# A hybrid conv and linear-attention layer with a ConvFFN: the next tile's scores ahead of this tile's mean of squares on TensorE, and loads and low parts in another order

## The chip, the cores and the metric

One Trainium2 chip, one of its cores. The metric is the device time of one execution in microseconds. The kernel is one program with an instruction list for each engine: TensorE (PE in the profile, PEld its weight loads), VectorE (DVE), ScalarE (ACT), GpSimd (POOL) and SyncE (SP, which issues the DMAs). The engines run side by side and meet only at semaphores; each takes its own list strictly in order.

## The reference, cut to what matters

2048 prompt rows and 64 sample rows of width 1024 go through one layer. All is float32.

```python
def mixer(xn, conv_prev, gla_prev, ...):
    bg, cg, h, q, k, v, gr, r = split(xn @ w_in)
    cv, conv_new = causal_dwconv(cg * h, conv_prev, conv_w)
    y_conv = rmsnorm(bg * cv, g_conv)
    logg = log_sigmoid(gr @ w_alpha + b_alpha) / 16
    o, gla_new = gla(q / 8, k, v, logg, gla_prev)     # 4 heads
    y_gla = rmsnorm(o, g_gla) * silu(r)
    return concat([y_conv, y_gla]) @ w_out, conv_new, gla_new

def gla(q, k, v, logg, s0):                            # chunks of 64 rows
    b = cumsum(logg)                                   # inside a chunk
    qt, kt, kd = q * exp(b), k * exp(-b), k * exp(b_last - b)
    att = where(mask, qt @ kt.T, 0)                    # the scores
    s_next = exp(b_last) * s + kd.T @ v
    o = att @ v + qt @ s                               # s: the state before the chunk

x = x + mixer(rmsnorm(x, norm1))
u = rmsnorm(x, norm2) @ w_up                           # 1024 x 5632
a, g = split(causal_dwconv(u, prev, ffn_conv_w))
x = x + (silu(g) * a) @ w_down                         # 2816 x 1024
y = rmsnorm(x, final_norm)
```

## The kernel before, in words

**Split products.** A float32 operand is written as a high part (rounded to the type that TensorE takes fast) and a low part (the rest). A product is three matmuls, high by high, low by high, high by low (L1617 to L1619). For a weight ScalarE makes the high part and GpSimd the low part; a part can't be used before both are there. `wq` holds such pairs for the large products, `w_hi` and `w_lo` those for v and for the output projection.

**Seven products for eight.** The projections of the mixer and w_up are computed with seven block products (numbered 0 to 6) over sums and differences of weight quarters; VectorE makes the four weight sums of a step in `sum_up` (tile `wu_sum`, L2080 to L2086) from `wu_raw`, and adds the products in PSUM together (`r_1` by ScalarE; `r_2` at L2538 and `r_3` at L2556 by VectorE). Product 5 of a step waits for `r_3`.

**Stages.** Rows come in three blocks of 768, 768 and 580 columns. For every block: the first norm and the turning of its tiles of 128 rows (x_n to xt_hi and xt_lo), the v product ("values"), 10 pairs of projections, of which gla runs beside, then the output projection, then the second norm. After the three blocks' mixers the ConvFFN runs for all three blocks in turn, 22 steps of 128 hidden rows each, 7 products a step, with the down products between them.

**gla beside the pairs.** `mix_events` places steps X, Y and Z of a tile t between pair products. On TensorE, X is `outputs_1(t)` (L1774 to L1781) and the gate product of t+1; Y is `outputs_2(t)` (L1788) and the cumulative sums of t+1 (L1744); Z is `mean_squares(t)` (L1796, one product of a ones matrix with `o_sq`) and `scores(t+1)` (L1752, and two transposes of k_end, L1757). For Z, ScalarE squares the output of t (`o_sq`, L1317), and VectorE's `decays(t+1)` makes q_exp, k_exp (L2185) and k_end. After `mean_squares`, ScalarE takes the root (`o_rs`, L1323 and L1326), and VectorE scales the tile (`gla_out`) behind `masked_scores(t+1)` (L2193). This happens 14 times with a next tile: 5, 5 and 4 in the three blocks.

**Output projection.** It is computed in two passes p of four weight units (slots) each. A pass starts with slot 0 for four row groups, slot 1 for the same four, and so on. The low parts of its rows come per head, for the two halves of a block's columns (`low_part`, L580). In pass 0 VectorE makes heads 0 and 1 (`y_lo_first`), GpSimd heads 2 and 3 between its low parts of the weight units (L554).

**Start and change of stages.** SP's list of loads sets what lands first; the rings take what SP issues in order. At the end of the last block's mixer the first FFN step is prepared: its products are split (L1110, L997), three split operands are stored for later blocks (`w_ops`), the weights of step 1 are loaded, then w_down's, and four x_ops tiles are stored, on which ScalarE's high part of w_down (`wd_hi`, L1192) waits, since it lies on the same memory.

Of the kernel before, what the change touches and what calls it, by code (L numbers as in the profile page):

```python
# [17 lines left out]
CJ = D_CONV // P  # L18
HEADS = 4
# [192 lines left out]
def build(nc, x_prompt, x_sample, state_conv, state_gla, state_ffn, w_in, w_alpha, b_alpha, conv_w,  # L212
          g_conv, g_gla, w_out, norm1, norm2, w_up, ffn_conv_w, w_down, final_norm,
          y_prompt, y_sample, conv_prompt, gla_prompt, ffn_prompt, conv_sample, gla_sample, ffn_sample):
    with ExitStack() as ctx:
# [182 lines left out]
        def mix_counts(b):  # L398
# [11 lines left out]
                "gla_y": nt, "y_hi": nch * HEADS + CJ, "y_lo": nch * (HEADS - 2) + CJ, "y_lo_first": 2 * nch,  # L410
# [226 lines left out]
        def _(sp):  # L637
# [92 lines left out]
            for b in range(NB):  # L730
# [12 lines left out]
                for t in range(0 if b else nt):  # L743
                    n1.wait(sp, "scaled", t - NX + 1)
                    load_x(t, b)
                    if t == 0:
                        load_gain(norm1[0])
                    if t < 2:
                        for slot in (2 * t, 2 * t + 1):
                            load_unit(sp, v_unit(b, slot))  # L750
                    if t == 2:
                        with nc.allow_non_contiguous_dma(reason="small parameters"):
                            sp.dma_start(raw_gr[:, :, :], w_in_v[:, :, C_GR:C_R]).then_inc(gr_loaded, 16)
                    if t == nt - 2:
                        load_parameters()
# [73 lines left out]
                if b == NB - 1:  # L829
# [3 lines left out]

                    for i in (1, 3, 4):
                        store_op(0, i)
                    sp.wait_ge(wu_lo, splits(0, 0, 5))
                    load_up(0, 1)
# [86 lines left out]
        def _(pool):  # L924
# [16 lines left out]
            for b in range(NB):  # L941
# [25 lines left out]
                def low_heads(chunk):  # L967
                    for n in range(2, HEADS):
                        mix.wait(pool, "y_hi", HEADS * chunk + n + 1)
                        mix.inc(low_part(pool, n, *CHUNKS[b][chunk]), "y_lo")  # L970

                low_unit(pool, out_unit(b, 0))
                low_unit(pool, out_unit(b, 1))
                low_heads(0)
                low_unit(pool, out_unit(b, 2))
                low_unit(pool, out_unit(b, 3))
                low_heads(1)
# [6 lines left out]
                if b == NB - 1:  # L984
                    mix.wait(pool, "y_lo", nch * (HEADS - 2) + CJ)
# [79 lines left out]
        def _(act):  # L1065
# [136 lines left out]
            act.wait_ge(consts_ready, 9)  # L1202
            for b in range(NB):
# [33 lines left out]
                if b == 0:  # L1237
                    for t in range(nt):
                        first_rstd(b, t)
                        if t >= 1:  # L1240
                            first_high(b, t - 1)
                        for slot in ((0, 1), (2, 3), ())[min(t, 2)]:
                            high_unit(act, v_unit(b, slot))
# [367 lines left out]
        def _(pe):  # L1611
# [29 lines left out]
            for b in range(NB):  # L1641
# [157 lines left out]
                for ev in mix_events(b):  # L1799
# [24 lines left out]
                    if ev[0] == "Z":  # L1824
                        mean_squares(t)
                        if more:
                            scores(t + 1)

                def out_group(p, n, slots):
# [9 lines left out]
                    for slot in slots:  # L1839
                        pe.wait_ge(lo_ready[slot], unit_index(b, "out", slot, p) + 1)  # L1840
                        if p:
                            mix.wait(pe, "y_lo", nch * (HEADS - 2) + slot + 1)
                        else:
                            mix.wait(pe, "y_lo_first" if slot < 2 else "y_lo", 2 * chunk_of_end(b, t) + slot % 2 + 1)
# [175 lines left out]
        def _(dve):  # L2020
# [67 lines left out]
            for b in range(NB):  # L2088
# [126 lines left out]
                def first_lows(c):  # L2215

                    for n in range(2):
                        mix.wait(dve, "y_hi", HEADS * c + n + 1)
                        mix.inc(low_part(dve, n, *CHUNKS[b][c]), "y_lo_first")
# [36 lines left out]
                def pair_event(p, i):  # L2256
# [51 lines left out]
                    if (p, i) == (NPAIR - 1, 4):  # L2308
                        first_lows(0)
# [39 lines left out]
                first_lows(nch - 1)  # L2349
# [7 lines left out]
                def add_out(p, j):  # L2357
# [4 lines left out]
                    if (p, t) == (0, max(TILES) // 2):  # L2362

                        mix.wait(dve, "y_lo", nch * (HEADS - 2))
# [151 lines left out]
            def ffn_step(b, f, par, more=True):  # L2516
# [22 lines left out]
                if edge == 0 and b == 0:  # L2539
                    sum_up(g + 1, 0)  # L2540
                    sum_up(g + 1, 1)
                    low_x(b, 5)
# [15 lines left out]
                if edge == 0 and b:  # L2558
# [7 lines left out]
                if edge == 0:  # L2566
                    low_x(b, 6)
                if at_last and b + 1 == NB - 1:
# [70 lines left out]
```

## Time and profile before

| | |
|---|---|
| median of 3 runs | 2353.17 us (2353.15 to 2356.1) |
| the profiled execution | 2356.82 us, its span 2355.1 us |
| TensorE matmuls | 2262.9 us busy, 96% |
| VectorE, ScalarE, GpSimd | 1700.4, 1002.6, 1209.8 us busy |
| granted TensorE clock, mean | 0.99 |
| DMA | 412.73 MB, mean 175 GB/s |

TensorE is busy in nearly the whole span, so the time is its work plus its idle stretches. Those lie in the first 20 us, in the mixer of each block, where the FFN starts (900 to 940 us), at the two changes of blocks in the FFN (about 1400 to 1470 and 1900 to 1980 us), and in the last 20 us.

### The profile page before, as it was taken

The page shows a single profiled execution, that of the slowest core. Times are in us where ns is not written, and L with a number is a line of the kernel's source. Part 1 is how long each engine was busy: PE and PEld are TensorE (multiplying, and loading weights), DVE is VectorE, ACT ScalarE, POOL GpSimd, SP SyncE. Part 2 cuts the span into 40 slices and gives each one's busy share as a digit, 9 for nine tenths or more (in the row PEclk, how much of TensorE's full clock was granted, in tenths as well). Part 3 has the DMA queues.
Part 4 walks back from the last instruction along what each step waited for, and adds up shares of the span by engine and source line. Part 5 has one row for each costly group of instructions (what it writes and reads, how often), then busy time and mean ns, then how long its engine had stood idle before and what let it go on. Part 6 is the DMA issues. An engine that isn't in the chain of part 4 may idle for free. (4 is left out here: it accounts for less than half of the span.)

```text
span 2355.1 us, 39571 instructions
## 1 busy us (share of the span) xinstructions
PE 2262.9 (96%) x12602; PEld 2072.1 (88%) x12602; DVE 1700.4 (72%) x2516; ACT 1002.6 (43%) x1957; POOL 1209.8 (51%) x1251
## 2 busy tenths in 40 slices
PE   7999999999999997999999998999999988999997
PEld 6998888988889976999999987999999977999996
DVE  6477775377554656989898887667676687788786
ACT  4544463343634454344444445333333335444343
POOL 2654732214532357787787865444444454555552
PEclk9999999999999998999999999999999999999999
DMA  3543446535366557544445476444444457555552
GB/s 124 192 166 133 162 159 226 170 117 183 130 232 206 175 211 268 179 151 160 163 157 177 152 259 224 148 158 149 151 147 142 151 171 251 196 187 196 194 188 102
DMA packets 264595, 412.73 MB, mean 175 GB/s; under 512 B 14108, under 2 KB 186993, under 8 KB 264497
## 3 DMA queue, kind: packets, MB, share of 16 engines
q1 hardware_dynamic: 264497, 411.45, 51.5%
q8 instruction: 58, 0.95, 0.2%
q14 instruction: 40, 0.33, 0.0%
HBM read 313.24 MB, written 98.16 MB: 175 GB/s over the span
## 5 line engine op out<-in xcount | busy, mean ns | idle before, releaser
L1617 PE MATMUL ps<-xo,wq 128*128 128x384 f32 (+1 forms) x1848 | 598.6, 324 | 24.8 <-POOL wq L997 10.6
L1618 PE MATMUL ps<-xo,wq 128*128 128x384 f32 (+1 forms) x1848 | 598.1, 324 | 0.0
L1619 PE MATMUL ps<-xo,wq 128*128 128x384 f32 (+1 forms) x1848 | 597.6, 323 | 0.0
L2471 DVE TENSOR_TENSOR resid<-resid,ps 128x512 f32<-128x512 f32 (+1 forms) x728 | 477.5, 681 | 73.8 <-PE ps L1619 45.2
L997 POOL TENSOR_TENSOR wq<-wu_raw,wq 128x256 fp32r<-128x256 f32 x396 | 384.4, 994 | 103.9 <-ACT wq L1110 103.8
L1617 PEld LDWEIGHTS ps<-xo,wq 128*128 128x128 f32 x1848 | 350.2, 189 | 46.6 <-issue 14.7
L1618 PEld LDWEIGHTS ps<-xo,wq 128*128 128x128 f32 x1848 | 350.6, 190 | 20.3
L1619 PEld LDWEIGHTS ps<-xo,wq 128*128 128x128 f32 x1848 | 351.0, 190 | 0.0
L2488 DVE SCALAR_TENSOR_TENSOR up_y<-up_u,params,up_y 128x768 f32<-128x768 f32 (+1 forms) x264 | 288.0, 1091 | 48.5 <-ACT up_y L1154 29.3
L519 POOL TENSOR_TENSOR wq<-wu_raw,wq 128x256 fp32r<-128x256 f32 x174 | 146.0, 861 | 300.9 <-ACT wq L1234 300.9
L1617 PE MATMUL ps<-wd_hi,hid_hi 128*128 128x512 f32 x704 | 277.0, 393 | 11.2 <-DVE resid L2471 11.2
L1619 PE MATMUL ps<-wd_lo,hid_hi 128*128 128x512 f32 x704 | 278.1, 395 | 0.0
L1618 PE MATMUL ps<-wd_hi,hid_lo 128*128 128x512 f32 x704 | 275.2, 391 | 0.0
L1027 POOL TENSOR_TENSOR wd_lo<-wd_raw,wd_hi 128x512 fp32r<-128x512 f32 x132 | 173.4, 1335 | 159.7 <-ACT wd_hi L1192 159.7
L1021 POOL TENSOR_TENSOR hid_lo<-up_y,hid_hi 128x384 fp32r<-128x384 f32 (+1 forms) x132 | 120.2, 932 | 167.5 <-ACT hid_hi L1182 167.5
L997 POOL TENSOR_TENSOR wq<-wu_sum,wq 128x256 fp32r<-128x256 f32 x176 | 159.1, 932 | 62.2 <-ACT wq L1110 62.2
L1617 PE MATMUL ps<-w_hi,xt_hi 128*128 128x512 f32 (+1 forms) x408 | 164.9, 404 | 6.4 <-POOL w_lo L554 3.1
L1154 ACT ACTIVATE up_y<-up_u,params 128x768 f32<-128x768 f32 (+1 forms) x132 | 116.9, 886 | 127.3 <-DVE up_u L2578 89.2
L1617 PE MATMUL ps<-xt_hi,wq 128*128 128x384 f32 (+1 forms) x480 | 158.8, 331 | 4.3 <-issue 2.9
L1618 PE MATMUL ps<-w_hi,xt_lo 128*128 128x512 f32 (+1 forms) x408 | 160.4, 393 | 0.0
L1619 PE MATMUL ps<-w_lo,xt_hi 128*128 128x512 f32 (+1 forms) x408 | 160.3, 393 | 0.0
L1619 PEld LDWEIGHTS ps<-wd_lo,hid_hi 128*128 128x128 f32 x704 | 132.9, 189 | 28.5
(246 smaller groups left out, 4232.0 us busy)
## 6 DMA issues: line engine op xcount, KB each, us to landing
wq<-w_ops SPq DMA_DIRECT2D x176, 512.0 KB, 4.5
wu_raw<-in_w_up_dram SPq DMA_DIRECT2D x89, 512.0 KB, 4.0
w_ops<-wq SPq DMA_DIRECT2D x88, 512.0 KB, 2.6
wq<-m_ops SPq DMA_DIRECT2D x80, 512.0 KB, 3.9
wd_raw<-in_w_down_dram SPq DMA_DIRECT2D x66, 512.0 KB, 5.3
wu_raw<-in_w_in_dram SPq DMA_DIRECT2D x40, 512.0 KB, 4.9
m_ops<-wq SPq DMA_DIRECT2D x40, 512.0 KB, 3.1
x_in<-in_x_prompt_dram SPq DMA_DIRECT2D x32, 512.0 KB, 5.6
```

What stands on the lines that cost most here:

```text
L519: last = eng.tensor_tensor(wq[:, at, 1, r], w[:, r], wq[:, at, 0, r].bitcast(F32), ALU.subtract)
L997: last = pool.tensor_tensor(wq[:, WQ_AT[i], 1, r], src[:, r], wq[:, WQ_AT[i], 0, r].bitcast(F32), ALU.subtract)
L1021: last = pool.tensor_tensor(hid_lo[:, par, r], up_y[:, 0, r], hid_hi[:, par, r].bitcast(F32), ALU.subtract)
L1027: last = pool.tensor_tensor(wd_lo[:, par, r], wd_raw[:, r], wd_hi[:, par, r].bitcast(F32), ALU.subtract)
L1154: return act.activation(up_y[:, m, 0:w], up_u[:, m, 2:2 + w], ACT.Copy, scale=params[:, FFN_TAP + 2, bass.ds(m * NF + f, 1)])
L1617: pe.matmul(out, lh, rh, start=(first and n == 0), stop=False, skip_group_check=skip)
L1618: pe.matmul(out, ll, rh, start=False, stop=False, skip_group_check=skip)
L1619: last = pe.matmul(out, lh, rl, start=False, stop=end, skip_group_check=skip)
L2471: last = dve.tensor_tensor(resid[0:m, t, s], resid[0:m, t, s], ps[0:m, bank, :], ALU.add)
L2488: dve.scalar_tensor_tensor(y, up_u[:, m, tap:tap + w], params[:, FFN_TAP + tap, bass.ds(m * NF + f, 1)], y, ALU.mult, ALU.add).then_inc(su ...
```

## The change

Five edits.

1. `scores(t+1)` stands before `mean_squares(t)` in step Z on TensorE.
2. The first loads: x tile 1 stands before the first v unit, and x tile 2 before the other three; ScalarE's high parts of the v units are spread behind the norm steps, and its wait for the constants stands behind the first table load.
3. Output projection: VectorE makes all four heads of the first half of the columns, GpSimd all four of the second half, behind the low parts of units 0 to 3.
4. End of the last mixer, on SP: the load of w_up for step 1 stands before the stores of the split operands.
5. First FFN step, on VectorE: the weight sums of step 1 stand behind r_3, the low parts of x operands 5 and 6 and the sum of the last quarter.

```diff
@@ SP, first loads
-                    if t < 2:
-                        for slot in (2 * t, 2 * t + 1):
-                            load_unit(sp, v_unit(b, slot))
+                    for slot in {1: (0,), 2: (1, 2, 3)}.get(t, ()):
+                        load_unit(sp, v_unit(b, slot))
@@ SP, end of the last mixer
+                    sp.wait_ge(wu_lo, splits(0, 0, 5))
+                    load_up(0, 1)
                     for i in (1, 3, 4):
                         store_op(0, i)
-                    sp.wait_ge(wu_lo, splits(0, 0, 5))
-                    load_up(0, 1)
                     second[b].wait(sp, "squared", nt)
                     load_down(0)
@@ GpSimd, low parts of the output projection
-                def low_heads(chunk):
-                    for n in range(2, HEADS):
-                        mix.wait(pool, "y_hi", HEADS * chunk + n + 1)
-                        mix.inc(low_part(pool, n, *CHUNKS[b][chunk]), "y_lo")
-                low_unit(pool, out_unit(b, 0))
-                low_unit(pool, out_unit(b, 1))
-                low_heads(0)
-                low_unit(pool, out_unit(b, 2))
-                low_unit(pool, out_unit(b, 3))
-                low_heads(1)
+                for n in range(4):
+                    low_unit(pool, out_unit(b, n))
+                for n in range(HEADS):
+                    mix.wait(pool, "y_hi", HEADS + n + 1)
+                    mix.inc(low_part(pool, n, *CHUNKS[b][1]), "y_lo")
@@ ScalarE, start
-            act.wait_ge(consts_ready, 9)
...
                 if b == 0:
+                    act.wait_ge(consts_ready, 9)
                     for t in range(nt):
                         first_rstd(b, t)
-                        if t >= 1:
+                        if t == 1:
+                            high_unit(act, v_unit(b, 0))
+                        if t >= 1 and t != 3:
                             first_high(b, t - 1)
-                        for slot in ((0, 1), (2, 3), ())[min(t, 2)]:
-                            high_unit(act, v_unit(b, slot))
+                        if t == 2:
+                            high_unit(act, v_unit(b, 1))
+                            first_high(b, 2)
+                            high_unit(act, v_unit(b, 2))
+                            high_unit(act, v_unit(b, 3))
@@ TensorE, step Z
                     if ev[0] == "Z":
-                        mean_squares(t)
                         if more:
                             scores(t + 1)
+                        mean_squares(t)
@@ VectorE, low parts
-                def first_lows(c):
-                    for n in range(2):
-                        mix.wait(dve, "y_hi", HEADS * c + n + 1)
-                        mix.inc(low_part(dve, n, *CHUNKS[b][c]), "y_lo_first")
+                def first_lows(heads):
+                    for n in heads:
+                        mix.wait(dve, "y_hi", n + 1)
+                        mix.inc(low_part(dve, n, *CHUNKS[b][0]), "y_lo_first")
...
-                first_lows(nch - 1)
+                first_lows((2, 3))
@@ VectorE, FFN step
                 dve.tensor_tensor(r_2[:, 0:h], ps[:, 1, 0:h], r_1[:, 0:h], ALU.add).then_inc(r2_read, 1)
-                if edge == 0 and b == 0:
-                    sum_up(g + 1, 0)
-                    sum_up(g + 1, 1)
-                    low_x(b, 5)
...
                 adds(3)
-                if edge == 0 and b:
+                if edge == 0:
                     low_x(b, 5)
...
                 if edge == 0:
                     low_x(b, 6)
+                if first_of_all:
+                    sum_up(g + 1, 0)
+                    sum_up(g + 1, 1)
```

TensorE's list at the first step Z of block 0 (o_sq is the squared output of this tile, q_exp, k_exp and k_end are of the next), with its - and +:

```order
-L1796 MATMUL ps<-o_sq,ones 128x512 [waits mix_o_squared]
 L1752 MATMUL ps<-q_exp,k_exp 128x128 [waits mix_att_read,mix_qk_exp]
 L1752 MATMUL ps<-q_exp,k_exp 128x128 x3
 L1757 MATMUL ps<-ident,k_end 128x128 [waits mix_qk_exp]
 L1757 MATMUL ps<-ident,k_end 128x128
+L1796 MATMUL ps<-o_sq,ones 128x512 [waits mix_o_squared]
```

The mean of squares moved behind the four score products and the two transposes.

VectorE's list in the first FFN step, before (r_66 is r_2, r_79 is r_3, wu_sum the weight sums of step 1, xo the low parts of x operands 5 and 6):

```order
L2538 TENSOR_TENSOR r_66<-ps,r_65 128x384 [waits r1_read,mix_p_done]
L2080 TENSOR_TENSOR wu_sum<-wu_raw 128x512 [waits wu_lo,mix_w_loaded1,mix_w_loaded0]
L2082 TENSOR_TENSOR wu_sum<-wu_sum,wu_raw 128x512 [waits mix_w_summed]
L2084 TENSOR_TENSOR wu_sum<-wu_raw 128x512
L2086 TENSOR_TENSOR wu_sum<-wu_raw,wu_sum 128x512 [waits mix_w_summed]
L2070 TENSOR_TENSOR xo<-xo_raw,xo 128x1536 [waits xo_high]
L2556 TENSOR_TENSOR r_79<-ps,r_65 128x384 [waits later_scaled,mix_p_done]
L2508 TENSOR_TENSOR up_u<-ps,r_79 128x384 [waits r3_read,mix_p_done]
L2070 TENSOR_TENSOR xo<-xo_raw,xo 128x1536 [waits xo_high]
L2578 TENSOR_TENSOR up_u<-ps,r_65 128x384 [waits mix_p_done]
```

and now:

```order
L2538 TENSOR_TENSOR r_66<-ps,r_65 128x384 [waits r1_read,mix_p_done]
L2552 TENSOR_TENSOR r_79<-ps,r_65 128x384 [waits later_scaled,mix_p_done]
L2070 TENSOR_TENSOR xo<-xo_raw,xo 128x1536 [waits xo_high]
L2508 TENSOR_TENSOR up_u<-ps,r_79 128x384 [waits r3_read,mix_p_done]
L2070 TENSOR_TENSOR xo<-xo_raw,xo 128x1536 [waits xo_high]
L2080 TENSOR_TENSOR wu_sum<-wu_raw 128x512 [waits wu_lo,mix_w_loaded1,mix_w_loaded0]
L2082 TENSOR_TENSOR wu_sum<-wu_sum,wu_raw 128x512 [waits mix_w_summed]
L2084 TENSOR_TENSOR wu_sum<-wu_raw 128x512
L2086 TENSOR_TENSOR wu_sum<-wu_raw,wu_sum 128x512 [waits mix_w_summed]
L2577 TENSOR_TENSOR up_u<-ps,r_65 128x384 [waits mix_p_done]
```

The four sums moved from before r_79 to behind the second low part; r_79 is now next after r_66.

SP's list at the same place, with its - and + (the stores w_ops are of step 0's operands, the loads wu_raw of step 1's weights):

```order
 L708 DMA xo_raw<-x_ops 128x1536 [waits mix_out_done]
 L708 DMA xo_raw<-x_ops 128x1536
+L656 DMA wu_raw<-in_w_up_dram 128x8x128 [waits wu_lo]
+L656 DMA wu_raw<-in_w_up_dram 128x8x128
 L695 DMA w_ops<-wq 128x1024 [waits wu_lo] x3
-L656 DMA wu_raw<-in_w_up_dram 128x8x128 [waits wu_lo]
-L656 DMA wu_raw<-in_w_up_dram 128x8x128
 L712 DMA wd_raw<-in_w_down_dram 128x1024 [waits later_squared]
```

The two loads stand before the three stores.

## Rows read from the trace of the kernel before

**Rows 1.** Who TensorE waited for, whole run: total us, times, longest.
```profile
PE ps L1617 <- POOL wq L997: 10.6, 1, 10.6
PE ps L1796 <- ACT o_sq L1317: 4.4, 4, 1.7
```

**Rows 2.** Timeline of the start: start us, us, engine, line, tiles [idle before].
```profile
10.66 1.06 ACT L1069 ACTIVATE squares<-x_in 128x1024 f32<-128x1024 f32 x1 [0.22 <-DMA x_in<-in_x_prompt_dram]
...
15.13 1.05 ACT L1069 ACTIVATE squares<-x_in 128x1024 f32<-128x1024 f32 x1
...
20.39 0.78 PE L1617 MATMUL ps<-w_hi,xt_hi 128*128 128x512 f32 x1
...
22.03 1.28 DVE L2038 TENSOR_TENSOR xt_lo<-ps,xt_hi 128x512 fp32r<-128x512 f32 x2
...
24.67 0.40 PE L1617 MATMUL ps<-w_hi,xt_hi 128*128 128x512 f32 x1
```

**Rows 3.** Timeline where output projections of block 0 and block 2 begin.
```profile
269.00 0.50 PE L1617 MATMUL ps<-w_hi,xt_hi 128*128 128x512 f32 x1 [0.53 <-POOL w_lo L554]
...
829.53 2.02 POOL L580 TENSOR_TENSOR xt_lo<-gla_y,xt_hi 128x290 fp32r<-128x290 f32 x2
831.52 5.94 POOL L554 TENSOR_TENSOR w_lo<-raw,w_hi 128x512 fp32r<-128x512 f32 x4
834.81 0.50 PE L1617 MATMUL ps<-w_hi,xt_hi 128*128 128x512 f32 x1 [2.08 <-POOL w_lo L554]
```

**Rows 4.** Stretches: from:to us, length, PE busy, PEclk, DMA share, GB/s.
```profile
835.86:839.27 3.41, 3.41 (x10) 0.50 1.01 410
907.60:921.20 13.60, 5.68 (x18) 0.50 1.06 369
918.00:934.00 16.00, 13.61 (x64) 0.82 1.05 381
```

**Rows 5.** Timeline of three of the 14 steps Z, all engines.
```profile
182.93 0.60 ACT L1317 ACTIVATE o_sq<-ps 128x512 f32<-128x512 f32 x1
183.58 1.12 PE L1796 MATMUL ps<-o_sq,ones 128*128 128x512 f32 x2 [1.73 <-ACT o_sq L1317]
184.05 0.43 DVE L2185 TENSOR_TENSOR k_exp<-k_exp,qk 128x256 f32<-128x256 f32 x1
184.54 1.15 PE L1752 MATMUL ps<-q_exp,k_exp 128*128 128x128 f32 x8
...
204.30 2.02 PE L1752 MATMUL ps<-q_exp,k_exp 128*128 128x128 f32 x8 [1.65 <-DVE k_exp L2185]
...
783.07 0.43 DVE L2185 TENSOR_TENSOR k_exp<-k_exp,qk 128x256 f32<-128x256 f32 x1
```

**Rows 6.** Timeline of the first two FFN steps, VectorE, TensorE and ScalarE.
```profile
909.87 0.90 DVE L2080 TENSOR_TENSOR wu_sum<-wu_raw 128x512 f32<-128x512 f32 x1 [10.90 <-DMA wu_raw<-in_w_up_dram]
...
914.83 0.54 DVE L2556 TENSOR_TENSOR r<-ps,r 128x384 f32<-128x384 f32 x1
...
915.52 0.66 PE L1617 MATMUL ps<-xo,wq 128*128 128x384 f32 x1 [10.62 <-POOL wq L997]
...
921.69 1.05 ACT L1192 ACTIVATE wd_hi<-wd_raw 128x1024 fp32r<-128x1024 f32 x1
...
931.15 0.41 PE L1617 MATMUL ps<-xo,wq 128*128 128x384 f32 x1 [2.39 <-DVE r L2538]
...
934.49 1.00 DVE L2080 TENSOR_TENSOR wu_sum<-wu_raw 128x512 f32<-128x512 f32 x1 [3.48 <-issue]
...
938.03 0.41 PE L1617 MATMUL ps<-xo,wq 128*128 128x384 f32 x1 [0.23 <-DVE r L2556]
```

**Rows 7.** SP's issues: the w_up loads of step 1, the last x_ops store (with us to landing).
```profile
899.12 2.69 SPq L656 DMA_DIRECT2D wu_raw<-in_w_up_dram  x2
...
910.18 1.39 SPq L845 DMA_DIRECT2D x_ops<-xl_a  x1
...
x_ops<-xl_a SPq DMA_DIRECT2D x1, 580.0 KB, 9.3
```

More of the change, by code:

```diff
@@ L409, in mix_counts @@
                 "state0": nt, "state1": full, "o_squared": nt, "o_mean": nt, "o_rs": 2 * nt, "gla_step": nt,
-                "gla_y": nt, "y_hi": nch * HEADS + CJ, "y_lo": nch * (HEADS - 2) + CJ, "y_lo_first": 2 * nch,
+                "gla_y": nt, "y_hi": nch * HEADS + CJ, "y_lo": HEADS + CJ, "y_lo_first": HEADS,
                 "csum": 2 * nch, "csq": nch, "cmean": nch, "crs": 2 * nch, "cy": CJ,
@@ L984, in _ @@
                 if b == NB - 1:
-                    mix.wait(pool, "y_lo", nch * (HEADS - 2) + CJ)
+                    mix.wait(pool, "y_lo", HEADS + CJ)
                     for t in (xl_a, xl_b):
@@ L1841, in out_group @@
                         if p:
-                            mix.wait(pe, "y_lo", nch * (HEADS - 2) + slot + 1)
+                            mix.wait(pe, "y_lo", HEADS + slot + 1)
                         else:
-                            mix.wait(pe, "y_lo_first" if slot < 2 else "y_lo", 2 * chunk_of_end(b, t) + slot % 2 + 1)
+                            mix.wait(pe, "y_lo" if chunk_of_end(b, t) else "y_lo_first", slot + 1)
                         k = (SLOTS * p + slot + HEADS) % KT
@@ L2308, in pair_event @@
                     if (p, i) == (NPAIR - 1, 4):
-                        first_lows(0)
+                        first_lows((0, 1))
                     if b == 0 and (p, i) == (0, 6):
@@ L2362, in add_out @@
                     if (p, t) == (0, max(TILES) // 2):
-                        mix.wait(dve, "y_lo", nch * (HEADS - 2))
+                        mix.wait(dve, "y_lo", HEADS)
                     for h in range(2):
```

## The prediction

> **What bounds the kernel now.** The page's first part comes first: matmuls fill 96% of the span, so the time is TensorE's work plus its idle stretches, and the change adds and removes no instruction. It can only fill or widen idle stretches, and what the granted clock does behind them. So the second view is the list of TensorE's waits [rows 1]: the start's, one of 10.6 us, those at the mean of squares. The timeline at each of the five places then says what ended the wait, and what would end it in the new order. Last come the stretches with their granted clock [rows 4]: behind some stalls TensorE runs at 0.50 (1.2 of 2.4 GHz) for 3.4 us or more, and half of such a busy stretch, 1.7 us, is lost on top of the stall.
>
> **Scores ahead of the mean of squares.** Nothing is removed. At a step Z the mean needs o_sq, the scores need k_exp. In all 14 places o_sq is ready first. At 183 us o_sq ends at 183.53 and k_exp at 184.48; the mean starts at 183.58, the scores at 184.54 [rows 5]. The mean, which holds TensorE for 184.54 - 183.58 = 0.96 us, fits into the wait for k_exp. In the new order the scores still start at 184.54, since neither k_exp nor what it hangs on comes from the mean, and the 0.96 us follow behind. Where both inputs are early (8 of the 14 places) the swap is neutral. In the other six (scores from 184.54, 204.30, 224.69, 497.11, 514.19 and 783.56 us; rows 5 hold the first two and the k_exp of the last) k_exp is what the scores start by, so each loses 0.9 to 0.96. One is given back: between 184 and 204 us VectorE has nearly no gap, so k_exp at 204.24 doesn't move when TensorE comes 0.96 later. In block 1 VectorE waits for TensorE between the two places, and the second loss comes on top. Sum: 5 x 0.95 = 4.7 us. On the clock: the stalls of 1.73 now become one of 2.7 at 184.5, and again at 497. A stall of 1.73 cost no clock, one of 2.08 did [rows 3, 4]. Of two possible low stretches (1.7 each) one is half absorbed before 204, and the low stretch that stands behind 204.30 now may fall away. I take +0.8. Together +5.5 us. Bounds: 0 (if VectorE, which masks the scores up to 1.3 us earlier, gains as much elsewhere) and 6 x 0.96 + 2 x 1.7 = 9.2. Behind the mean wait ScalarE's root, its copy of the turned k_end and its next high parts, on VectorE the scaling; these come up to 1.3 us later. The next outputs_1 needs the scaled tile; it waited 0.7 and 0.9 us in two places, so a few tenths more, inside the range.
>
> **Low parts of the output projection.** In block 2 GpSimd spends 2.02 us on two head parts before the low part of unit 2, whose two halves take half of 5.94 us; TensorE waits 2.08 for it [rows 3]. With the heads gone from there (VectorE has them, 0.8 to 1.6 us each, at a time when it waits for nobody), unit 2 starts at 829.75, since its high part is there, and is done at 832.8 where TensorE arrives at 832.73. Unit 3 ends near 835.8 and is wanted at 835.6. So 0.35 of the 2.08 stays, 1.7 goes. With it goes the low clock behind it, 3.41 us wholly busy at 0.50 [rows 4], 1.7 us. Blocks 0 and 1 lose their waits of 0.53 and 0.50. GpSimd's four parts of the second half end near 839 us and are first wanted at about that time for head 0 alone, for head 3 2 us later. Sum -(1.7 + 1.7 + 0.5 + 0.5) = -4.4. The next wait, 1.07 at 860.6, hangs on a chain that starts at TensorE and moves along. Bounds -5 and -1.5 (the clock falls all the same).
> By the Trainium skill (GPSIMD Engine Reference, section 1, Specifications) GpSimd's SBUF interfaces are shared with VectorE, and two-input operations contend. The trace agrees: 5.94 / 4 = 1.49 us a half beside VectorE's work here. VectorE's own low parts now fall on the same microseconds; if they stretched GpSimd's halves to 1.7, unit 3 would be 0.9 later and this term -3.5.
>
> **The first loads.** The third tile is what the start is late by: its square begins at 15.13, the second's at 10.66 on its landing [rows 2]. In the new list they stand two and three places earlier, at (15.13 - 10.66) / 3 = 1.5 us a place. So the third square starts at about 11.9, behind the second one and its unit, the third x_n follows 1.8 later at 13.7, is turned by 17.2 at the cold clock, and the first v product starts at 17.3 instead of 20.39. But TensorE's third group (24.67 now) needs the low part of tile 2 (22.03 to 23.3 now), and VectorE makes that behind the scaling of tile 3, whose square ScalarE now reaches only behind units 1 to 3: 19.8 us, so x_n at 21.6 to 22.9 and the low part at 24.2. The third group starts at about 24.25, 0.4 us earlier, behind a new wait of nearly 3 us, which can cost up to 1.7 of clock. +0.7, bounds -1.5 and +2.
>
> **The first FFN steps.** The 10.62 us at 915.52 are put down to GpSimd, but product 5 waits for r_3, which VectorE makes at 914.83 behind the sums, which waited 10.90 for the second load of w_up [rows 6]. In the new order r_3 comes at 903, product 5 at 905.9, and the load lands near 904. This stall goes. What is late next: ScalarE's wd_hi (921.69, no wait now) waits for the last x_ops store, which lands at 910.18 + 9.3 = 919.5 [rows 6, 7]. ScalarE would be there at 913. The order of loads and stores ahead doesn't change their sum, so it still waits until 919.5; silu, the taps, r_1 and r_2 are queued behind it. So product 2 of step 1 waits some 8 us instead, and product 3 (931.15) starts at 928.2. Then product 5 of step 1: it starts at 938.03, 0.23 us after TensorE is there, by r_3, behind the sums, which begin at 934.49 when the load for step 2 has landed. That load stands behind some 20 other transfers issued from 899 on (the two loads, four stores, w_down, four x_ops, six rows of x, three stores), and the rings are full all the while (share 1.05 from 918 to 934 [rows 4]), with nothing taken from them. So product 5 starts at 938.03 as before and the whole gain is spent waiting, near 5 us in one stall. Two costs come with it: that stall takes the clock, and its low stretch lies where TensorE has work: 1.7, and up to half of the 5.7 us which stayed low behind 915.52, 2.8 [rows 4]. And in 895 to 899 no stores fill the rings, since they now stand behind a load that waits for GpSimd until 899: 0 to 2 us of DMA time, I take 0.8. Sum +1.9 + 0.8 = +2.7. Bounds -10 (the full stall gone) and +5.
>
> **Sum.** 5.5 - 4.4 + 0.7 + 2.7 = +4.5 us. Against the profiled execution, 2356.8 (span 2355.1 and 1.7 around it), that is 2361.3. That execution lay 3.7 above the median of the runs; carried to the median, 2353.2 + 4.5 = 2357.7.
>
> **Rivals.**
> (a) The swap costs nearly nothing: VectorE is the engine that TensorE waits for in the mixer, and earlier masks help it as much as later means hurt. For it: where TensorE and VectorE take turns, a later TensorE is absorbed, as before 204.30. Against: five places without that. Then 2357.7 - 4.7 = 2353.0, no change.
> (b) The FFN start pays, and the kernel is faster: the step-2 load lands early enough. The place is product 5 of step 1, the price r_3's start there less r_3's start now. It decides from the point where the sums start before 931 instead of at 934.49. Then the low stretch goes too, and the sum is 5.5 - 4.4 + 0.7 - 7 = -5: 2348. Against it stands the full ring share.
> By the Trainium skill (DMA: Bandwidth & Descriptors, "Two DMAs through the same engine are not ordered") reads and writes of an engine are separate queues and a later one may complete first, so loads might pass the stores ahead of them; by that rule the outcome is this one, 2348. The trace shows no such passing: of the loads issued behind stores from 899.12 on, the second landed only at 909.8, by the sums' start [rows 6, 7].
> (c) Both new stalls in the mixer and the one at the FFN take the clock in full and the rings lose 2 us: 4.5 + 3.5 + 2 = +10: 2363.
> (d) The change doesn't do what it says at its name: the scores aren't earlier in any of the six places. That is the forecast's own case.
>
> **Chances.** Forecast 0.50, (a) 0.22, (b) 0.12, (c) 0.16. About 0.2%, 4.7 us, is what a measurement of this kernel tells from no change. The forecast's own range is 2354 to 2361, and lies on both sides of 2357.9: half of it slower, half the same. Slower: 0.25 + 0.16 + 0.05 = 0.46. Faster: 0.10 of (b) and 0.03 of (a) and the rest: 0.14. Same 0.40. The range for 8 in 10: 2350.5 to 2363.
>
> **What would show it.** Right: in the profile after, the scores of those five places start when k_exp ends and the means follow without a wait; waits of L1752 for k_exp are 8 us or more, those of L1796 for o_sq none. The wait for w_lo in the output projection falls from 3.1 to below 1. Product 5 of the first FFN step starts 9 us earlier, ScalarE's wd_hi waits for a DMA, and the sums of step 2 start no earlier than now against the issue of the first load of w_up for step 1, 35.4 us (934.49 less 899.12). Wrong: these sums start more than 2 us earlier, or fewer than four places lose the mean's 0.9 us.

## The result, and the profile after

| | before | changed |
|---|---|---|
| median of 7 runs each, same chip | 2353.45 us (2351.69 to 2360.06) | 2363.66 us (2361.14 to 2365.22) |
| ratio, 95% interval | | 1.0033 (1.0023 to 1.0043) |
| profiled execution, its span | 2356.82, 2355.1 | 2364.02, 2362.3 |
| granted clock, mean | 0.990 | 0.987 |

The change makes the kernel slower by 0.33%, 7.8 us (5.4 to 10.1); the two medians of seven lie 10.2 apart. The forecast was 2357.7 and slower by 4.5. The median lies 0.7 above the upper end of the range for 8 in 10, 2363.0, and 2.7 above that of the forecast's own range, 2361. In the later comparisons, with 15 to 35 runs of the kernel before each, the medians of before were 2355.1 to 2355.5, so the base of 2353.2 was probably some 2 us low; in this comparison itself it was 2353.45.

TensorE's waits in the changed kernel (who waited, for whom: total us, times, longest), against [rows 1]:

```profile
PE ps L1752 <- DVE k_exp L2185: 11.9, 6, 3.2
PE ps L1617 <- ACT r L1111: 9.2, 2, 8.8
PE ps L1617 <- DVE r L2552: 7.5, 3, 4.7
PE ps L1617 <- DVE xt_lo L2038: 3.6, 1, 3.6
PE ps L1788 <- DVE gla_s L2203: 1.3, 1, 1.3
PE ps L1617 <- POOL w_lo L554: 0.6, 2, 0.4
```

The wait of 10.6 for GpSimd and the 4.4 for o_sq are gone, the 3.1 for w_lo shrank to 0.6. In their place stand one of 8.8 for ScalarE, one of 4.7 for r_3 (3.1 in all before, 7.5 now), 11.9 in six places for k_exp, and two that were not there: 3.6 for the low part of tile 2 and 1.3 for gla_s.

Where the time went is read by taking one instruction after another that both timelines have, and subtracting its start before from its start after. The difference changes only where the change did something:

| TensorE instruction (start before) | after less before, us | what lies between it and the row above |
|---|---|---|
| turn of the last tile, 36.02 | +2.3 | the start |
| first scores, 130.16 | +2.6 | first pairs |
| outputs of tile 1, 153.81 | +6.6 | steps Y and Z of tile 0 |
| last outputs of block 0 with a next tile, 228.88 | +8.5 | four steps Z |
| first scores of block 1, 444.64 | +7.2 | output projection 0 |
| outputs, 536.23 | +11.3 | steps Z of block 1 |
| first scores of block 2, 733.89 | +11.0 | output projection 1 |
| outputs, 805.75 | +12.2 | steps Z of block 2 |
| last turn, 897.72 | +8.9 | output projection 2 |
| product 5 of FFN step 1, 938.03 | +8.8 | FFN start |
| FFN, 1410.03 | +10.8 | the clock behind it |
| last stall, 2333.23 | +8.2 | the two changes of blocks |
| end | +7.2 | the last 20 us |

The start, the changed kernel's timeline, against [rows 2]:

```profile
11.46 1.06 ACT L1064 ACTIVATE squares<-x_in 128x1024 f32<-128x1024 f32 x1
...
16.29 0.78 PE L1617 MATMUL ps<-w_hi,xt_hi 128*128 128x512 f32 x1
...
23.07 1.27 DVE L2038 TENSOR_TENSOR xt_lo<-ps,xt_hi 128x512 fp32r<-128x512 f32 x2
24.40 0.80 PE L1617 MATMUL ps<-w_hi,xt_hi 128*128 128x512 f32 x1 [3.61 <-DVE xt_lo L2038]
```

The third square starts at 11.46 (15.13 before) and the first v product at 16.29 (20.39), but the third group only at 24.40 (24.67): TensorE has its first two groups done and stands 3.61 us. What that costs in clock, and the same at three other stalls, is in the stretches at the granted clock of 0.50, 1.2 of 2.4 GHz (from:to us, length, then busy time of PE, PEld, DVE, ACT and POOL, clock, DMA share, GB/s):

```profile
22.92:29.75 6.83, 5.35 (x17) 4.47 (x18) 3.59 (x6) 1.27 (x3) 1.77 (x2) 0.50 0.35 92
145.80:152.63 6.83, 5.71 (x19) 5.71 (x20) 6.02 (x13) 4.92 (x13) 4.42 (x6) 0.50 0.39 128
504.20:507.61 3.41, 3.29 (x13) 2.78 (x13) 3.31 (x8) 0.00 (x0) 0.00 (x0) 0.50 0.13 52
944.52:951.35 6.83, 4.56 (x14) 4.49 (x15) 3.62 (x7) 3.51 (x6) 5.59 (x8) 0.50 0.26 100
```

Half of each busy time, 2.7, 2.9, 1.6 and 2.3 us, is what the clock can have cost; by the start differences it was 2.6, 2.6, 1.5 and 2.1. The first explains +2.3 from a third group that starts 0.3 earlier. Behind a single stall stood low stretches of up to 6.83 us; the forecast had reckoned with 3.41 for each new one.

A step Z with a late k_exp, and two outputs behind a step Z, against [rows 5]:

```profile
189.53 0.60 ACT L1317 ACTIVATE o_sq<-ps 128x512 f32<-128x512 f32 x1
190.65 0.42 DVE L2185 TENSOR_TENSOR k_exp<-k_exp,qk 128x256 f32<-128x256 f32 x1
191.13 1.16 PE L1752 MATMUL ps<-q_exp,k_exp 128*128 128x128 f32 x8 [2.68 <-DVE k_exp L2185]
192.35 1.02 PE L1796 MATMUL ps<-o_sq,ones 128*128 128x512 f32 x2
...
210.90 2.08 PE L1752 MATMUL ps<-q_exp,k_exp 128*128 128x128 f32 x8 [3.16 <-DVE k_exp L2185]
...
504.31 2.08 PE L1752 MATMUL ps<-q_exp,k_exp 128*128 128x128 f32 x8 [2.68 <-DVE k_exp L2185]
...
547.55 1.13 PE L1774 MATMUL ps<-v_tok,k_end_t 128*128 128x128 f32 x8 [0.96 <-DVE gla_y L2213]
```

o_sq is ready at 190.13, k_exp at 191.07: TensorE waits through the time in which it used to do the mean. The last line is a cost that stands behind the mean and not at the scores: VectorE's scaling comes later, and the outputs wait for it.

The FFN start, timeline, against [rows 6]:

```profile
911.77 0.56 DVE L2552 TENSOR_TENSOR r<-ps,r 128x384 f32<-128x384 f32 x1 [3.88 <-PE ps L1619]
...
914.09 0.41 PE L1617 MATMUL ps<-xo,wq 128*128 128x384 f32 x1 [0.28 <-issue]
...
928.52 1.06 ACT L1187 ACTIVATE wd_hi<-wd_raw 128x1024 fp32r<-128x1024 f32 x1 [6.88 <-DMA x_ops<-xl_a]
...
931.84 0.66 PE L1617 MATMUL ps<-xo,wq 128*128 128x384 f32 x1 [8.84 <-ACT r L1111]
...
943.27 0.98 DVE L2080 TENSOR_TENSOR wu_sum<-wu_raw 128x512 f32<-128x512 f32 x1 [7.03 <-issue]
...
946.79 0.66 PE L1617 MATMUL ps<-xo,wq 128*128 128x384 f32 x1 [4.72 <-DVE r L2552]
```

Against the 8.9 us by which everything is late here, r_3 comes 12 us earlier and the stall of 10.62 is gone; the time is then spent at wd_hi and at product 5 of step 1. SP's list at that place, against [rows 7]:

```profile
908.04 1.01 SPq L656 DMA_DIRECT2D wu_raw<-in_w_up_dram  x2
909.09 3.70 SPq L695 DMA_DIRECT2D w_ops<-wq  x3
...
920.79 5.55 SPq L722 DMA_DIRECT2D resid<-x_mid  x6
926.38 1.38 SPq L695 DMA_DIRECT2D w_ops<-wq  x3
927.81 8.21 SPq L656 DMA_DIRECT2D wu_raw<-in_w_up_dram  x2
```

The sums of step 2 start 943.27 - 908.04 = 35.2 us behind the issue of the step-1 load; the forecast said no earlier than 35.4. Six loads of resid rows and three stores stand directly ahead of the step-2 load. That is the handle of an experiment below.

Output projection of block 2, against [rows 3]:

```profile
838.92 9.16 POOL L554 TENSOR_TENSOR w_lo<-raw,w_hi 128x512 fp32r<-128x512 f32 x6 [0.33 <-ACT w_hi L547]
...
848.14 0.50 PE L1617 MATMUL ps<-w_hi,xt_hi 128*128 128x512 f32 x1 [0.21 <-POOL w_lo L554]
```

Six halves of weight units run through without a head part between, 1.53 us each, and TensorE waits 0.21 where it waited 2.08.

### The profile page after: what moved, and what is told of

Read it like the earlier page. It is cut to its first block and busy times, and to the rows that moved or that the text cites. A ratio compares the mean times of both kernels' runs of the same rounds, so it can differ in the third digit from the quotient of the medians.

```text
span 2362.3 us, 39572 instructions
## 1 busy us (share of the span) xinstructions
PE 2266.7 (96%) x12602; PEld 2076.0 (88%) x12602; DVE 1700.7 (72%) x2516; ACT 1003.4 (42%) x1957; POOL 1207.3 (51%) x1251
```

## The experiments

Twelve kernels, each timed in five rounds beside the kernel before. A difference in us is (ratio - 1) x 2355, with its 95% interval. Each kernel was profiled once. In the diffs, `...` stands for lines left out; of the first four kernels' diffs only the lines that name the edit are shown.

**The five edits apart.** In each of these four kernels only the edit named is made.

```diff
# e1_swap
-                        mean_squares(t)
                         if more:
                             scores(t + 1)
+                        mean_squares(t)
```


> The kernel before with edit 1 alone (scores ahead of the mean of squares). Theory, from the profile of the changed kernel: block 0's steps Z cost 1.9 us, block 1's 4.1 (1.5 of it clock), block 2's 1.2, so +7 us, 5.5 at least; scores wait for k_exp some 11 us in six places, the mean never waits for o_sq. Rival: the steps Z absorb the later mean (each place that loses 0.9 us gives it back at the next outputs), and the loss seen in the changed kernel is clock and late loads that the other edits brought: then within 2 us of before.

```diff
# e2_start: first loads, ScalarE's start
+                    for slot in {1: (0,), 2: (1, 2, 3)}.get(t, ()):
+                        load_unit(sp, v_unit(b, slot))
...
```


> The kernel before with edit 2 alone (first loads, ScalarE's start). Theory: the third group waits 3.6 us for the low part of tile 2 and the clock falls on it, +2.3 us up to 60 us. Whether the wait for gla_s near 140 us (4.0 us with its clock in the changed kernel) belongs to this edit is what the run tells: if the late landing of the weights there comes from the shifted start, +6.5 us in all; if that landing is a thing of one execution, +2.3 and no wait for gla_s over 0.3 us. Rival: the start is neutral, within 1 us.

```diff
# e3_lows: GpSimd; VectorE makes all four heads of the first half
+                for n in range(4):
+                    low_unit(pool, out_unit(b, n))
+                for n in range(HEADS):
+                    mix.wait(pool, "y_hi", HEADS + n + 1)
...
```


> The kernel before with edit 3 alone (low parts of the output projection). Theory: -1.2, -0.4 and -3.2 us in the three blocks as in the changed kernel, -4.9 in all; TensorE's waits for w_lo fall from 3.1 to about 0.6 us, the low clock at 836 us goes. Rival: in the changed kernel part of that gain was time lent by the later steps Z (the projection had more slack because TensorE came late); then -2.5 or less.

```diff
# e4_ffn: SP and VectorE
+                    load_up(0, 1)
                     for i in (1, 3, 4):
                         store_op(0, i)
...
+                if first_of_all:
+                    sum_up(g + 1, 0)
+                    sum_up(g + 1, 1)
...
```


> The kernel before with edits 4 and 5 alone (first FFN steps). Theory: product 5 of step 0 starts 10 us earlier, product 2 of step 1 waits 8.8 us for ScalarE behind wd_hi, product 5 of step 1 waits 4.7 us and starts when it did before; the clock then costs 2 us: +2. Rival 1: the whole is neutral, since the clock falls where it falls, 0 +- 1. Rival 2: without the later arrival of the changed kernel the rings are emptier and the step-2 load lands early: -5 or better.

| edit | forecast | alone, by the ratio | ratio |
|---|---|---|---|
| 1, scores first | +5.5 | +6.8 (4.2 to 9.4) | 1.0029 |
| 2, first loads | +0.7 | +2.4 (0 to 4.7) | 1.0010 |
| 3, low parts | -4.4 | -5.4 (-8.0 to -3.1) | 0.9977 |
| 4 and 5, FFN start | +2.7 | +0.9 (-1.6 to +3.5) | 1.0004 |
| sum | +4.5 | +4.7 | changed kernel: 1.0033, +7.8 |

All four point the way that was forecast, though the interval of edits 4 and 5 holds zero, and that of edit 2 ends at it. The sum of the four is that of the forecast, and in part by luck: two terms were short, by 1.3 and 1.7, two too dear, by 1.0 and 1.8, and these cancel. The whole is 3 us over the sum; with intervals of 2 to 3 us to either side on each of the five numbers, that is no sign of an interaction. The waits are those expected: 11.2 us in six places for k_exp in e1_swap, 3.7 for the low part of tile 2 in e2_start with the clock low behind it, 0.8 for w_lo in e3_lows, 8.5 for ScalarE and 5.0 for r_3 in e4_ffn.

These four also answer a question on the changed kernel's profile. The wait for gla_s near 142 us, which the profile of before does not have, stands in the kernel of e4_ffn, which is the kernel before up to 890 us (its timeline):

```profile
138.04 0.69 DVE L2123 TENSOR_TENSOR wu_sum<-wu_raw 128x512 f32<-128x512 f32 x1 [1.55 <-DMA wu_raw<-in_w_in_dram]
140.59 1.40 DVE L2203 SCALAR_TENSOR_TENSOR gla_s<-gla_s,decay,ps 64x128 f32<-64x128 f32 x4
142.04 0.71 PE L1788 MATMUL ps<-q_exp,gla_s 128*128 128x128 f32 x4 [0.98 <-DVE gla_s L2203]
```

VectorE's sums wait for a load of w_in, and gla_s stands behind them. In e2_start, of which no wait over 0.3 us was expected if this was a thing of one execution, it stands too, with 1.54 us. Of the 14 kernels profiled once each, 11 have this wait near 142 us, with 1.0 to 1.7 us; in 5 of the 11 the clock fell on it, in two of them (e8_ffn_resid and e12_ffn_dve, which are the kernel before up to 890 us) for 6.8 us as in the changed kernel. So the +4.0 between 131 and 154 us is not put down to the change: 1.4 of it is a wait that most executions of either kernel seem to have, 2.6 a clock that falls on it in some. The profile of before happened to have neither. In the same way the 2.08 for w_lo at 834.81 stands in 4 of the 9 profiles with GpSimd's old order (before, e1, e4, e12: 2.1 to 2.2) and is 0.5 in the other five.

**Where the swap costs.** Between the steps of gla, pair products are spread by rounding; in blocks 0 and 1 one product stands between Y and Z of tiles 2 and 3, and two at the other tiles. That is where k_exp is latest.

```diff
# e5_even
-                upto = len(products) - LEFT - rest + (n + 1) * rest // len(steps)
+                upto = g + STEP_PRODUCTS[b][n]
...
+STEP_PRODUCTS = [[1, 2, 2] * 5 + [2, 2, 2], [1, 2, 2] * 5 + [2, 2, 2], [2, 2, 2, 2, 3, 2, 2, 2, 2, 2, 3, 2, 2, 3]]
```


> The kernel before, the swap not made, with the pair products spread otherwise between the gla steps: two products stand between every Y and Z of blocks 0 and 1 (before: one at Y2 and Y3), and three at Y3 of block 2, taken from behind the X of the same tile. Theory (k_exp is late because only one product covers VectorE's and ScalarE's chain behind the cumulative sums): the waits for o_sq (4.4 us) and k_exp (1.7) go, three short waits for lg of 0.4 each come in each of two blocks; -3 us. Rival (VectorE's whole queue is late, whatever stands between): the waits stay or turn up at the step behind, within 1 us of before.

Measured: 0.9987 (0.9978 to 0.9996), -3.1 us. The second kernel is this one with the scores ahead.

```diff
# e6_even_swap: e5_even and
-                        mean_squares(t)
                         if more:
                             scores(t + 1)
+                        mean_squares(t)
```


> The same spread, and the scores ahead of the mean of squares. Theory (the swap costs the mean's 0.9 us only where k_exp is late): with k_exp early everywhere the swap costs nothing here, so within 1 us of the run without it, against 6.8 us on the old spread; waits of the scores for k_exp below 1.5 us in all. Rival (the swap costs because everything behind the mean, the root, the turned copy of k_end, the scaling, comes later): it costs 4 us or more on this spread too, as waits for gla_y or at the outputs.

Measured: 0.9992 (0.9982 to 1.0002), -1.9 us. So by the two ratios the swap costs 1.2 us on the even spread, against 6.8 on the old one; by the two kernels' medians, 2351.78 and 2355.29, it costs 3.5, and the 1 us of the theory isn't kept. TensorE's waits of the two, e5_even first:

```profile
PE ps L1745 <- DVE lg L2170: 6.3, 10, 1.5
PE ps L1775 <- DVE gla_y L2214: 1.9, 4, 0.9
PE ps L1797 <- ACT o_sq L1318: 0.8, 2, 0.5
```

```profile
PE ps L1753 <- DVE k_exp L2186: 4.5, 4, 1.4
PE ps L1775 <- DVE gla_y L2214: 1.1, 2, 0.7
```

The spread takes o_sq from 4.4 to 0.8 and k_exp away, and adds 3.3 at lg (2.4 expected). The swap brings 4.5 for k_exp back, where 1.5 was expected at most: k_exp is a little late in four places even here. It gives up 0.8 + 0.8 at o_sq and gla_y, so its price in this pair of profiles is 2.9 us, between the 1.2 and the 3.5. By each of the three it is under the 6.8, and under the rival's 4. The step's price goes with how late k_exp is: 11.2 us of waits for it on the old spread, 4.5 here.

**The start.** Edit 2 and one more step.

```diff
# e7_start_low: VectorE
+                        if t == 3:
+                            first_low(b, 2)
                         first_scale(b, t)
-                        if t:
+                        if t and t != 3:
                             first_low(b, t - 1)
```


> The kernel before with edit 2 and one more step: VectorE makes the low part of tile 2 ahead of the scaling of tile 3. Theory (the 3.6 us wait of the third group and the low clock behind it are all that eats the earlier start): the third group starts at 20.7 us instead of 24.4, no low clock at 23 us, and turns of tile 3 at 22.3; -4 us against before in profile and median, -6.5 against edit 2 alone. Rival (the weights' low parts or the landing of x tiles 3 to 5 bound the first 40 us): TensorE waits at a later group for as long, within 1 us of before.

Measured: 0.9976 (0.9965 to 0.9986), -5.7 us. The wait of 3.6 is gone and the clock stays up; instead TensorE waits 1.06 for the next tile (timeline):

```profile
17.24 0.69 DVE L2043 TENSOR_TENSOR xt_lo<-ps,xt_hi 128x512 fp32r<-128x512 f32 x1 [0.16 <-ACT xt_hi L1079]
...
23.25 1.07 PE L1632 MATMUL ps<-ident,x_n 128*128 128x128 f32 x8 [1.06 <-DVE x_n L2029]
```

By the start differences the start itself gives 2.7 us, less than the 4.0 expected. The profile gains 1.6 more behind 204 us, where that of before had this low stretch (columns as above), and 1.5 in the last output projection, where before waited 2.08 us:

```profile
204.39:207.80 3.41, 3.41 (x14) 3.41 (x15) 2.72 (x7) 0.76 (x2) 0.44 (x1) 0.50 0.86 289
```

No edit of this kernel lies at either place, and e2_start, whose edit lies at the start too, has neither the low stretch nor the 2.08. So what of the 5.7 (3.3 to 8.2) belongs to the start beyond 2.7 is not shown. The diagnosis stands: with the one low part ahead, the edit that cost 2.4 pays.

**The FFN start.** Edits 4 and 5, and six loads moved in SP's list.

```diff
# e8_ffn_resid: SP, first FFN step
-                if b == 0 and edge == 0:
-                    for t in range(TILES[0]):
-                        load_resid(0, t)
...
                     load_up(*then)
+                if b == 0 and edge == 0:
+                    for t in range(TILES[0]):
+                        load_resid(0, t)
```


> The kernel before with edits 4 and 5, and the six loads of resid rows behind the w_up load of step 2 instead of ahead of it. Theory (the step-2 load lands late because the rings are full with what stands ahead of it): the sums of step 2 start 5 to 9 us earlier, product 5 of step 1 no longer waits (5.0 us), the low clock behind it goes (2): -6 against edits 4 and 5 alone, -4.5 against before; the 8.5 us wait for ScalarE stays, since the x_ops stores are ahead of both. Rival 1 (the load is bound by its own issue or by the split that frees its memory): nothing changes. Rival 2: the resid rows now land late and the first sum into resid holds the down products, which takes back what is won.

Measured: 0.9979 (0.9968 to 0.9989), -4.9 us, 5.8 better than with edits 4 and 5 alone. SP's issues and VectorE's first sum of step 2:

```profile
902.64 1.01 SPq L656 DMA_DIRECT2D wu_raw<-in_w_up_dram  x2
...
922.10 1.26 SPq L656 DMA_DIRECT2D wu_raw<-in_w_up_dram  x2
923.40 4.46 SPq L722 DMA_DIRECT2D resid<-x_mid  x6
```

```profile
929.25 0.68 DVE L2080 TENSOR_TENSOR wu_sum<-wu_raw 128x512 f32<-128x512 f32 x1
...
935.00 0.68 DVE L2471 TENSOR_TENSOR resid<-resid,ps 128x512 f32<-128x512 f32 x1
```

The sums start 26.6 us behind the issue of the step-1 load instead of 35.2, and product 5 of step 1 waits for nobody. The resid rows are there when they are wanted. Between the last turn (897.72 in before) and 1410.03 this kernel gains 5.4 us on before by the start differences, where e4_ffn loses 1.5.

Edit 5 without edit 4:

```diff
# e12_ffn_dve: VectorE's part of edit 5 only; SP as before
...
+                if first_of_all:
+                    sum_up(g + 1, 0)
+                    sum_up(g + 1, 1)
```


> The kernel before with edit 5 alone (VectorE's sums of step 1 behind r_3), SP's list as before. Theory (edit 5 moves the stall, edit 4 only costs 0.8 us of idle rings): TensorE's waits in the first FFN steps as with both edits (8.5 us for ScalarE, 5 us for r_3), the time within 1 us of theirs. Rival (the earlier w_up load of edit 4 does something): the split of step 1 ends later, product 5 of step 0 goes as early, but later stalls grow by 1 us or more.

Measured: 1.0007 (0.9998 to 1.0016), +1.6 us; with edit 4 it was +0.9. TensorE's stalls (timeline), this kernel and then e4_ffn:

```profile
919.20 0.44 PE L1617 MATMUL ps<-xo,wq 128*128 128x384 f32 x1 [1.30 <-POOL wq L997]
928.52 0.66 PE L1617 MATMUL ps<-xo,wq 128*128 128x384 f32 x1 [6.97 <-ACT r L1116]
...
943.44 0.66 PE L1617 MATMUL ps<-xo,wq 128*128 128x384 f32 x1 [5.27 <-DVE r L2552]
```

```profile
922.88 0.66 PE L1617 MATMUL ps<-xo,wq 128*128 128x384 f32 x1 [8.52 <-ACT r L1116]
...
937.97 0.66 PE L1617 MATMUL ps<-xo,wq 128*128 128x384 f32 x1 [5.05 <-DVE r L2552]
```

1.30 + 6.97 + 5.27 = 13.5 against 8.52 + 5.05 = 13.6: edit 4 only moves 1.3 us from one wait to another. The waits show nothing of its cost of 0.8 in the forecast; the two times, each 2 to 3 us uncertain, can't tell.

**All that paid together**, with and without the swap, and one more order of stores.

```diff
# e9_best: before, edits 2 to 5, and the diffs of e5_even, e7_start_low and e8_ffn_resid
```


> Everything that paid, and no swap: edits 2 to 5, the low part of tile 2 ahead of the scaling of tile 3, the even spread of products between the gla steps, the resid loads behind the step-2 load. Theory (the places are far apart and add up): measured alone these gave 5.2 (edit 3), 5.7 (start), 3.1 (spread) and 4.9 us (edits 4 and 5 with the resid loads), 18.9 together; the low clock that each took with it can be the same one twice, so -15 to -19. Rival: they share the few low stretches of the clock that a profile has, and give -10.

Measured: 2342.73 us against 2355.42, 0.9945 (0.9932 to 0.9959), -13.0 us (9.7 to 16.0): faster than both kernels. That lies between the theory's 15 to 19 and the rival's 10, and the interval holds the 10 and the 15. The single gains sum to 19.1; each interval is 2 to 3 us to either side, so how much is overlap isn't settled.

```diff
# e10_best_swap: e9_best and
-                        mean_squares(t)
                         if more:
                             scores(t + 1)
+                        mean_squares(t)
```


> The same with the scores ahead of the mean of squares. Theory (the swap costs only what k_exp is late by): on the even spread it cost 1.2 us by the medians' ratios, so 0 to 2.5 us here. Rival: 5 us or more, as on the old spread.

Measured: 2345.51 us, 0.9958 (0.9944 to 0.9971), -9.9 us. The swap costs 3.1 us by the ratios, a little above the 0 to 2.5 expected, and again under the 6.8, though with five runs of each kernel the intervals meet. TensorE waits 4.6 us for k_exp in four places, as in e6_even_swap.

```diff
# e11_best_xops: e9_best and, SP behind load_up(0, 1)
-                    for i in (1, 3, 4):
-                        store_op(0, i)
-                    second[b].wait(sp, "squared", nt)
-                    load_down(0)
-                    store_op(0, 6)
+                    store_op(0, 1)
...                  # the four x_ops stores
+                    second[b].wait(sp, "squared", nt)
+                    load_down(0)
+                    for i in (3, 4, 6):
+                        store_op(0, i)
```


> The kernel of all that paid, and the four x_ops stores ahead of w_down's load and of the stores of split operands 3, 4 and 6. Theory (ScalarE's wd_hi waits for the last x_ops store, and TensorE's product 2 of step 1 waits 7.4 us behind it): wd_hi starts 4 to 6 us earlier and TensorE's wait shrinks by as much; product 5 of step 1 waits again for the step-2 load, so -3 of that stays. Rival (the rings take the same bytes in the same time, and ScalarE's splits of step 1 now wait for the stores of operands 3 and 4): no gain, or 1 to 3 us slower.

Measured: 2346.59 us, 0.9954 (0.9941 to 0.9968), -10.8 us: 2.1 slower than e9_best by the ratios, 3.9 by the medians of five runs each. The theory's gain isn't there, and the wait that the rival named is. ScalarE's list (timeline):

```profile
910.47 0.63 ACT L1107 ACTIVATE wq<-wu_sum 128x512 fp32r<-128x512 f32 x1 [7.03 <-DMA w_ops<-wq]
...
913.57 1.04 ACT L1189 ACTIVATE wd_hi<-wd_raw 128x1024 fp32r<-128x1024 f32 x1
```

wd_hi no longer waits for x_ops, but ScalarE stands 7.03 us ahead of it, at a split that may not overwrite an operand until its store has landed. TensorE's wait for ScalarE grows from 7.4 to 11.4.

## Why the forecast was right in kind and short in size

**The swap, +5.5: right, 1.3 short.** All six places lose the mean, scores wait for k_exp 11.9 us (8 or more was said) and the mean waits for nobody. By the start differences the six lost 0.83, 0.77, 1.09, 0.93, 0.86 and 0.85, and the first was absorbed ahead of the second (210.90) as forecast: 4.5 against 4.7. One low stretch cost 1.5 where 0.8 was reckoned for all; in e1_swap both stalls named in the forecast have one (at 188.10 and 502.13). The step that failed is the seventh place, 0.8 us at 547.55: the term had put "a few tenths more" for waits behind the mean, at a step Z where both inputs are early and the swap was called neutral. Rival (a), that it costs nothing, has the lower bound of 4.2 us against it.

**The low parts, -4.4: right.** -1.2, -0.3 and -3.3 in the three blocks by the start differences, -4.8 in all; -5.4 alone. The contention that the Trainium skill states (GPSIMD Engine Reference, section 1, Specifications) did not stretch GpSimd's halves to 1.7: the six took 1.53 on average beside VectorE's work, where others in the kernel before took 1.29 with VectorE idle. That the 2.08 stands in only four of nine profiles would make the mean gain smaller than the profile's; the interval of e3_lows doesn't show it.

**The first loads, +0.7: right in each time, the clock mis-sized.** Third square 11.5 (forecast 11.9), low part of tile 2 to 24.3 (24.2), third group 24.40 (24.25), its wait 3.6 (nearly 3). The step that failed is "up to 1.7 of clock": it is 2.6, since the low stretch is 6.83 us long. The +0.7 took only about 1.1 of clock against the 0.4 gained, with no reason given for less than 1.7. The first v product comes at 16.29, a microsecond earlier than forecast, which only makes the stall longer.

**The FFN start, +2.7: right in each wait, 1.8 too dear.** Less the 8.9 us of shift, r_3 came at 902.9 (903), wd_hi at 919.6 (919.5), product 5 of step 1 at 937.9 (938.03). The clock took 2.1 (1.9), but the working names 1.7 and up to 2.8 and does not say how they make 1.9, so that this agrees tells little. The 0.8 for idle rings is not seen in the waits (e12_ffn_dve). That the step-2 load hangs on what stands ahead of it was argued from the ring's share alone; e8_ffn_resid shows it. The Trainium skill (DMA: Bandwidth & Descriptors, "Two DMAs through the same engine are not ordered") has it that when a later descriptor completes an earlier one need not have finished writing. Here that brought no early load: with the resid loads ahead the sums started 35.2 us behind the issue of the step-1 load, with them behind it 26.6.

**What the sum lacked.** 2.6 us of clock and 1.4 us of wait at 140 to 154 us, which one execution of before did not have; 2.6 and 1.0 us came back at the changes of blocks and at the end, where neither kernel's list differs. Of the 7.2 between the two spans, these make up +4.0 and -3.6. The number of rival (c), 2363, is nearest to the median. Of its mechanism, this profile has the clock at the FFN's stall and at one of the two in the mixer (504.31, not 191.13); its 2 us of rings are not seen.

## What to carry to other kernels

Two instructions of one engine that wait for different inputs are ordered by which input comes first: the earlier one fits into the wait for the later. If both are early the order itself costs nothing, but what stands behind the one that is now second can (0.8 us at 547.55). So before swapping, list at each place when both inputs are there, and look at what frees the later input: the pair products spread so that k_exp comes earlier were worth 3.1 us, the swap cost 6.8.
When a stall is taken away by moving an instruction, look at what the instructions behind it wait for. At the FFN start these were two transfers further back in the queue, and the edit paid (7 us at that place) only when loads that nobody wanted yet were moved behind the second.
A short stall seen, or missing, in one profile is a sample: of the two met here, one of 2.1 us stood in 4 of 9 profiles and one of 1.0 to 1.7 in 11 of 14, and a low stretch of the clock behind the second in 5.

## What the runs showed of the hardware

- The same stall takes the clock or doesn't: of 11 profiles with 1.0 to 1.7 us of wait for gla_s and 1.5 for lg 2 us later, the granted clock fell to 0.50 in five. Stretches at 0.50 were of 3.41, 6.83 or 10.24 us in the changed kernel, and the four that were looked at cost 1.5 to 2.6 us. A stall of 2.68 us for k_exp had one behind it at 504.31 and none at 191.13; in e1_swap both places had one.
- VectorE's two-input sums of 128x512 took 0.69 us alone and up to 1.50 beside GpSimd's splits, so sums that start earlier can also run slower. It is what the Trainium skill says of the two engines' shared interfaces (GPSIMD Engine Reference, section 1, Specifications). A sum of step 2 in e8_ffn_resid, timeline:

```profile
931.31 1.50 DVE L2084 TENSOR_TENSOR wu_sum<-wu_raw 128x512 f32<-128x512 f32 x1
```
